# Inverting the key norms as one column per chunk and head in a recurrent-scan kernel, with its helper jobs moved and a fifth job place added

## The chip, the cores and the metric

The kernel runs as one launch on one core of a Trainium2 chip, all arithmetic in fp32. The metric is the device time of that launch in microseconds (us), the median over the runs shown. The engines are called TensorE (PE in the profile; PEld is its weight load), VectorE (DVE), ScalarE (ACT), GpSimd (POOL) and SyncE (SP, which issues most DMAs).

## The reference, cut to what matters

One layer of a hybrid backbone over 128 context and 1024 latent tokens (1152 in all) of width 1024: a modulated RMSNorm and an input projection, two parallel mixers (RWKV-7 scans in both directions, and a pooling mixer), an output projection, an expert-choice mixture of 16 experts, a last norm. The change is in the scans:

```python
kk = heads(k * k_k)
kk = kk / jnp.maximum(jnp.sqrt(jnp.sum(kk * kk, axis=-1, keepdims=True)), 1e-12)
k_dir = heads(k[:, :, None, :] * (1.0 + (a - 1.0) * k_a))
...
sa = jnp.einsum('bhvk,bhk->bhv', s, kk_t)
s = (s * w_t[:, :, None, :] - sa[..., None] * b_t[:, :, None, :]
     + v_t[..., None] * k_t[:, :, None, :])          # b_t = kk * a
```

`kk` is the key of each token and head (8 heads of 64), divided by its own length: one number per token and head, shared by 64 channels.

## The kernel before, in words

Five phases run one after the other, with a barrier between them: `project_phase` (to about 405 us of the span), `scan_phase` (about 405 to 1168), `output_phase`, `expert_phase` (the long one) and `final_phase`. Only `scan_phase` is touched.

**Layout.** Channels lie on partitions: a *channel tile* t (0 to 3) is 128 partitions = 2 heads of 64, with the 1152 tokens in the free dimension, worked on in three *pieces* c of 384 tokens (`piece(c)`). Two big buffers, `wide` and `set1`, hold the prepared tensors of even and odd tiles (`bufs(t)`), so that tile t+1 is prepared while tile t is scanned.

**The scan rounds.** The scan is done by chunks of 64 tokens (`CH`); 128 tokens are a *cell*, 9 cells per tile, 36 in all, done two at a time in 18 *rounds* p = 0 to 17. The engines have hand-written programs in which each round has the same skeleton: a triangular matrix is inverted in six levels, `lv` = 0 to 5. Per level and cell TensorE does `inv_x`, ScalarE copies it (`take_x`, L1038), TensorE does `inv_t`, and VectorE adds it to `tw` (`take_t`, L1249 for level 0, L1254, and L1257 for level 5). GpSimd makes the masked matrix of each level (`level`, L882) and `tw` at the round's start (`begin_tt`, L889). Between the levels stand the other steps of the two old cells (`wu`, `fin`, `step`, `y0`) and the first ones of the two next (`ab`, `masked`, L1239).

**The side work.** Three lists fill the gaps of the rounds. *Jobs* are matmuls of 384 columns with their evictions, at up to four places (`spot(p, k)`, k = 0 to 3: places 0 and 1 in level 4, 2 and 3 in level 5); `jobs(p, k)` says which. `between(p, q)` on VectorE, ScalarE and GpSimd holds the element-wise steps after level q. The preparation of tile t = 1, 2, 3 begins in round `PREP[t]` = 0, 4, 8 and takes rounds r = 0 to 3 counted from there, so that rounds 1, 5, 9 are its r = 1, rounds 2, 6, 10 its r = 2, rounds 3, 7, 11 its r = 3. The output norm of tile 0, 1, 2 begins in round `NORM[t]` = 6, 10, 14. Tile 0 is prepared in a *prologue* ahead of round 0 (p = -1), and tile 3 is normed in a *tail* (`TAIL`). A job's PSUM banks are G[0] and G[1]; TensorE waits for all earlier evictions before a job (`evicted`), and once more at the next round's start before `wu`.

**The key norm before**, per piece: ScalarE squares k (`square`, L991); job `kk` sums the squares of each head with a block of ones, so that the sum stands in all 64 rows of the head; ScalarE takes the square root (L999) into a 128x384 tile in `kr[:, 1, 1]`; VectorE bounds it from below (`floor`, L1189), inverts all 128x384 numbers (`unit`, L1197), multiplies key, k_k and inverse (L1199), and multiplies the rate pair `nb` by it (L1202). In the rounds `floor` stands at (r, q) = (1, 5), (2, 1), (2, 4) and `unit` at (2, 2), (2, 3), (2, 5). Behind them: the exponentials (`exps`, L1009 to L1015, two halves per piece at (2, 3), (2, 4), (2, 5), (3, 1), (3, 2), (3, 3)), VectorE's `keys` (L1215, L1216) and `factors` (L1226 to L1234), GpSimd's `kr` (L901), `kd` (L894) and `bonus` (L907, L909). The output norm has a like step, `spread` (L1209), a reciprocal of 128x384.

## Time and profile before

| | us |
|---|---|
| median of 3 runs (lowest, highest) | 3024.35 (3022.92, 3027.27) |
| the profiled execution, own time | 3028.03 |
| its span, first to last instruction | 3026.2 |
| TensorE busy in the span | 2715.8 (90%) |
| VectorE busy | 1214.7 (40%) |
| ScalarE, GpSimd busy | 568.8, 569.1 (19% each) |
| mean granted TensorE clock | 0.956 of 2.4 GHz |

The page gives busy sums over the whole span. The scan phase is a quarter of it, so its share is read from windows of the trace: busy time of each engine in a stretch, and how long a round lasts.

### The profile page before, as it was taken

The numbers are of one execution on the slowest core, as the hardware profiler recorded it, in microseconds if no ns is written. First come the engines' busy times: TensorE is split into PE (matmuls) and PEld (weight loads), VectorE is DVE, ScalarE is ACT, GpSimd is POOL, SyncE is SP. The second block draws the span as 40 slices with busy tenths as digits, with TensorE's granted clock in tenths as the row PEclk, the third lists the DMA queues.
The fourth block names the chain that finished last, engine by engine and source line by source line (L and its number), as shares of the span: only waits on it lengthen the run. The fifth ranks groups of instructions, "written<-read, shape, count | busy, mean of one in ns | idle before, by whom it ended". The sixth has DMA issues, their size and how long they took to land. (4 is left out here: it accounts for less than half of the span.)

```text
span 3026.2 us, 74869 instructions
## 1 busy us (share of the span) xinstructions
PE 2715.8 (90%) x32716; PEld 2389.9 (79%) x32716; DVE 1214.7 (40%) x3032; ACT 568.8 (19%) x1406; POOL 569.1 (19%) x571
## 2 busy tenths in 40 slices
...
DMA packets 235257, 517.92 MB, mean 171 GB/s; under 512 B 9853, under 2 KB 42877, under 8 KB 234938
## 3 DMA queue, kind: packets, MB, share of 16 engines
...
## 5 line engine op out<-in xcount | busy, mean ns | idle before, releaser
L2275 PE MATMUL ps_h<-xT,w1c 128*128 128x144 f32 x4096 | 547.1, 287 | 1.3 <-ACT xT L2081 1.3
L2275 PE MATMUL ps_h<-xT,w3c 128*128 128x144 f32 x4096 | 544.3, 286 | 0.0
L2275 PEld LDWEIGHTS ps_h<-xT,w1c 128*128 128x128 f32 x4096 | 520.4, 191 | 1.7 <-ACT xT L2081 1.7
L2275 PEld LDWEIGHTS ps_h<-xT,w3c 128*128 128x128 f32 x4096 | 519.9, 190 | 0.0
L2285 PE MATMUL ps_ye<-he,w2c 128*128 128x144 f32 x4096 | 512.3, 286 | 0.0
L2285 PEld LDWEIGHTS ps_ye<-he,w2c 128*128 128x128 f32 x4096 | 505.9, 190 | 0.0
L2230 DVE TENSOR_TENSOR u<-ps_h,sig 128x144 f32<-128x144 f32 x256 | 78.8, 308 | 887.8 <-ACT sig L2112 887.8
L563 PE MATMUL front_bank<-wide,win 128*128 128x384 f32 x912 | 298.9, 490 | 2.0 <-DVE wide L447 2.0
L563 PEld LDWEIGHTS front_bank<-wide,win 128*128 128x128 f32 x912 | 173.8, 191 | 128.2 <-issue 9.9
L2112 ACT ACTIVATE sig<-ps_h 128x144 f32<-128x144 f32 x256 | 74.4, 291 | 1065.8 <-PE ps_h L2275 1065.8
L2143 POOL DMA_INDIRECT acc<-ys,idx_s x16 | 25.8, 1615 | 1002.8 <-ACT ye_p L2101 872.0
L882 POOL TENSOR_TENSOR lm<-am,cst 128x256 f32<-128x256 f32 x216 | 164.7, 782 | 261.9 <-DVE am L1239 155.2
L1413 PE MATMUL bank<-xw,tw 64*64 64x64 f32 x2304 | 147.1, 221 | 28.6 <-ACT xw L1038 13.8
L1413 PE MATMUL bank<-tw,xw 64*64 64x64 f32 x2880 | 166.3, 220 | 6.4 <-issue 5.3
L1254 DVE TENSOR_TENSOR tw<-bank,tw 128x512 f32<-128x512 f32 x144 | 98.8, 690 | 181.0 <-PE bank L1413 180.7
L1413 PEld LDWEIGHTS bank<-tw,xw 64*64 64x64 f32 x2880 | 150.3, 137 | 14.7 <-issue 11.2
L1413 PEld LDWEIGHTS bank<-xw,tw 64*64 64x64 f32 x2304 | 131.4, 136 | 37.3 <-ACT xw L1038 18.2
L2137 POOL DMA_INDIRECT xs<-h,idx_s x17 | 17.0, 1001 | 706.0 <-DVE idx_p L2200 706.0
L1413 PE MATMUL bank<-tw,lm 64*64 64x64 f32 x2880 | 114.9, 225 | 28.5 <-DVE tw L1249 16.1
L1413 PEld LDWEIGHTS bank<-tw,lm 64*64 64x64 f32 x2880 | 105.7, 141 | 37.1 <-issue 32.5
L2181 DVE TENSOR_SCALAR_CACHE_REDUCE after<-prow,pcol 128x128 f32<-128x128 f32 (+2 forms) x153 | 115.6, 756 | 0.1
L487 DVE SCALAR_TENSOR_TENSOR mod_sum<-ada,silu_c,mod_sum 128x512 f32<-128x512 f32 x112 | 106.7, 953 | 5.5 <-DVE mod_sum L487 1.6
...
## 6 DMA issues: line engine op xcount, KB each, us to landing
...
```

Of the source, the lines that this page charges most:

```text
L487: mc(eng.scalar_tensor_tensor(out, ada[:, h, k], c, out, ALU.mult, ALU.add))
L563: ins = eng.matmul(ps_p[b][c][:, 0:PIECE], win[:, b, k], hT[:, k, c * PIECE:(c + 1) * PIECE], start=(k == 0), stop=(k == KT - 1))
L882: eng.tensor_tensor(lm[:, b, lv % 2].rearrange("p (d h) c -> p d h c", d=2), am[:, n % 4, :, :, 2], lvl[:, :, lv].unsqueeze(2).to_broadcas ...
L1254: ins = eng.tensor_tensor(flat, INV[b][:], flat, ALU.add)
L1413: return eng.matmul(out, a, b, start=start, stop=stop, skip_group_check=True)
L2112: eng.activation(sig[:, f % 2], ps_h[f % 2][:, 0:SLOTS], ACT.Sigmoid).then_inc(sig_done, 1)
L2137: eng.indirect_dma_start(xs[:], None, io["h2"], bass.IndirectOffsetOnAxis(ap=idx_s[:, 0], axis=0)).then_inc(gathered, 16)
L2143: eng.indirect_dma_start(io["acc"], bass.IndirectOffsetOnAxis(ap=idx_s[:, 1], axis=0), ys[:], None, compute_op=ALU.add).then_inc(scattered ...
L2181: eng.tensor_scalar(after[:, 0:hi - me], prow[:, me:hi], p, None, ALU.is_gt, ALU.add, accum_out=cnts[:, t, 1:2])
L2230: eng.tensor_tensor(u[:, f % 2], ps_h[f % 2][:, 0:SLOTS], sig[:, f % 2], ALU.mult).then_inc(u_done, 1)
L2275: ins = eng.matmul(ps_h[g % 2][:, off:off + SLOTS], w[:, b, k, f * P:(f + 1) * P], xT[:, k], start=(k == 0), stop=(k == KT - 1))
L2285: ins = eng.matmul(yps(k), w2c[:, b, f, k * P:(k + 1) * P], he[:, b, f], start=(c == 0 and f == 0 and k % 3 == 0), stop=(c == NCHUNK - 1 a ...
```

## The change

**Norm.** A new job `ks`, one per tile, replaces the three `kk`: 36 matmuls, each with the squares of one chunk and head as stationary 64x64 operand and one column of ones as moving operand, so that the sums of a chunk stand as one column of 64. ScalarE takes two roots of 128x9 into `rt` (128x2x9), VectorE bounds and inverts `rt` once (`invert`). Job `kb`, one per piece, spreads the inverses back: 12 matmuls whose stationary operand is one column of `rt` repeated 64 times and whose moving operand is `eye`. `unit` then multiplies key, k_k and the PSUM result in two instructions of 128x192, and `nb` as before. The squares go to `kr[:, 0, 1]` or, for t > 1, to `kdt`.

**Places.** A round gets a fifth place, `spot(p, 4)`, after place 3, on banks G[2] and G[3]. The jobs, `kd`, `kr`, `exps`, `normed`, `deviation` and `spread` move as the diff shows. `spread` becomes three reciprocals of 128x128.

```diff
         if p == -1:
-            for lo, name, t in ((0, "w", 0), (3, "a", 0), (6, "kk", 0), (9, "w", 1)):
+            for lo, num, name, t in ((0, 1, "ks", 0), (1, 3, "w", 0), (4, 3, "a", 0), (7, 3, "kb", 0), (10, 3, "w", 1)):
...
-            if r == 0 and k < 3 and t > 1:
-                found.append(("w", t, k))
-            for name, spots in (("a", ((0, 3), (1, 0), (1, 1))), ("kk", ((1, 2), (1, 3), (2, 0))),
-                                ("bonus", ((3, 1), (3, 2), (3, 3)))):
+            spots = {"ks": ((0, 0),), "w": ((0, 1), (0, 2), (0, 3)) if t > 1 else (), "a": ((1, 0), (1, 1), (1, 2)),
+                     "kb": ((1, 3), (2, 0), (2, 1)), "bonus": ((3, 1), (3, 2), (3, 3))}
...
-            e = 4 if t < 2 else 2
-            gate = ((3, 2), (3, 3), (5, 0)) if t < 2 else ((3, 0), (3, 2), (3, 3))
-            for name, spots in (("mean", ((0, 2), (0, 3), (1, 0))), ("var", ((1, 1), (1, 2), (e, 1))), ("gate", gate)):
+            spots = {"mean": ((0, 2), (0, 3), (1, 0)), "var": ((1, 1), (1, 2), (2, 4)),
+                     "gate": ((3, 4), (3, 4), (4, 4)) if t < 2 else ((3, 2), (3, 3), (3, 4))}
...
@@ gpsimd, between @@
-                if (r, q) in ((1, 1), (1, 5), (2, 0)):
-                    kd(t, ((1, 1), (1, 5), (2, 0)).index((r, q)))
-                if (r, q) in ((2, 5), (3, 1), (3, 3)):
-                    kr(t, ((2, 5), (3, 1), (3, 3)).index((r, q)))
+                if (r, q) in ((1, 4), (1, 5), (2, 0)):
+                    kd(t, ((1, 4), (1, 5), (2, 0)).index((r, q)))
+                if (r, q) in ((2, 4), (3, 0), (3, 2)):
+                    kr(t, ((2, 4), (3, 0), (3, 2)).index((r, q)))
...
-                spots = ((2, 0), (2, 1), (5 if t < 2 else 3, 0))
+                spots = ((2, 1), (2, 3), (3, 2))
                 if (r, q) in spots:
                     normed(t, spots.index((r, q)))
@@ scalar, between @@
-                if (r, q) in ((1, 3), (1, 4)):
-                    for c in ((0,), (1, 2))[q - 3]:
-                        square(t, c)
-                spots = ((2, 3), (2, 4), (2, 5), (3, 1), (3, 2), (3, 3))
+                if r == 0 and q <= 3:
+                    square(t, q - 1)
+                spots = ((2, 2), (2, 3), (2, 4), (2, 5), (3, 1), (3, 2))
...
-                spots = ((0, 5), (1, 1), (3, 5) if t < 2 else (2, 1))
+                spots = ((0, 5), (1, 1), (2, 3))
                 if (r, q) in spots:
                     deviation(t, spots.index((r, q)))
@@ vector @@
-        def floor(t, c):
-            x = bufs(t)[0][:, 1, 1, piece(c)]
-            eng.wait_ge(job_s, taken[("kk", t, c)])
-            eng.tensor_scalar(x, x, 1e-12, None, ALU.max).then_inc(floor_v, 1)
+        def invert(t):
+            eng.wait_ge(job_s, taken[("ks", t, 0)])
+            eng.tensor_scalar(rt[:], rt[:], 1e-12, None, ALU.max).then_inc(floor_v, 1)
+            eng.wait_ge(floor_v, 2 * t + 1)
+            eng.reciprocal(rt[:], rt[:]).then_inc(floor_v, 1)
...
             eng.wait_ge(kd_p, 3 * t + c + 1)
-            eng.wait_ge(floor_v, 3 * t + c + 1)
-            x = kr[:, 1, 1, piece(c)]
-            eng.reciprocal(x, x).then_inc(unit_v, 1)
-            eng.wait_ge(unit_v, 9 * t + 3 * c + 1)
-            eng.scalar_tensor_tensor(kx, kx, head(t, "k_k"), x, ALU.mult, ALU.mult).then_inc(unit_v, 1)
-            eng.wait_ge(unit_v, 9 * t + 3 * c + 2)
+            eng.wait_ge(job_p, order_pe[("kb", t, c)])
+            k3 = kx.rearrange("p (b c x) -> p b c x", c=2, x=CH)
+            for m, b in enumerate(bank_of("kb", t, c)):
+                eng.scalar_tensor_tensor(k3[:, :, m], k3[:, :, m], head(t, "k_k"), b[:, 0:PIECE // 2].rearrange("p (b x) -> p b x", x=CH),
+                                         ALU.mult, ALU.mult).then_inc(job_v, 1)
...
-            eng.reciprocal(x, x).then_inc(spread_v, 1)
+            for j in range(3):
+                ins = eng.reciprocal(x[:, j * P:(j + 1) * P], x[:, j * P:(j + 1) * P])
+            ins.then_inc(spread_v, 1)
...
-                spots = ((1, 5), (2, 1), (4 if t < 2 else 2, 5))
+                spots = ((1, 5), (2, 2), (3, 1))
                 if (r, q) in spots:
                     spread(t, spots.index((r, q)))
@@ tensor, job @@
+            elif name == "ks":
+                eng.wait_ge(square_s, 3 * t + 3)
+                for j in range(NCH):
+                    for h in range(2):
+                        ins = mm(b[h][H[j % 2], j // 2:j // 2 + 1], squares(t)[H[h], j * CH:(j + 1) * CH], blk[H[h], h * HS:h * HS + 1])
+            elif name == "kb":
+                eng.wait_ge(floor_v, 2 * t + 2)
+                for j in range(NB // 3):
+                    for m in range(2):
+                        for h in range(2):
+                            i = c * (NB // 3) + j
+                            ins = mm(b[m][H[h], j * CH:(j + 1) * CH], rt[H[m], h, i:i + 1].to_broadcast([HS, HS]), eye[H[m]])
@@ tensor, spot @@
-            else:
+            elif k < 4:
                 evicted(p, k)
                 if k == 0:
                     eng.wait_ge(d_s, 2 * p + 2)
+            else:
+                eng.wait_ge(am_v, min(2 * p + 4, NCELL))
```

Two places show how the instructions move. First VectorE in round 2 (r = 2 of tile 1, buffer `set`), from the step that follows `take_f` of the second old cell to the end of the round. `zs` is the scan state, `am` the masked matrix of a next cell. Before:

```order
L1197 RECIPROCAL set<-set 128x384
L1199 SCALAR_TENSOR_TENSOR z<-z,par,set 128x384
L1202 SCALAR_TENSOR_TENSOR set<-set,z 128x2x384
L1287 SCALAR_TENSOR_TENSOR zs<-bank,fc,mrn 128x64 x2
L1254 TENSOR_TENSOR tw<-bank,tw 128x512 x2
L1239 TENSOR_TENSOR am<-bank,cst 128x2x256 x2
L1197 RECIPROCAL set<-set 128x384
L1199 SCALAR_TENSOR_TENSOR z<-z,par,set 128x384
L1202 SCALAR_TENSOR_TENSOR set<-set,z 128x2x384
```

The same place in the changed program:

```order
L1300 SCALAR_TENSOR_TENSOR zs<-bank,fc,mrn 128x64 x2
L1267 TENSOR_TENSOR tw<-bank,tw 128x512 x2
L1252 TENSOR_TENSOR am<-bank,cst 128x2x256 x2
L1267 TENSOR_TENSOR tw<-bank,tw 128x512 x2
L1300 SCALAR_TENSOR_TENSOR zs<-bank,fc,mrn 128x64 x2
L1209 SCALAR_TENSOR_TENSOR z<-z,par,bank 128x3x64 x2
L1213 SCALAR_TENSOR_TENSOR set<-set,z 128x2x384
L1252 TENSOR_TENSOR am<-bank,cst 128x2x256 x2
L1209 SCALAR_TENSOR_TENSOR z<-z,par,bank 128x3x64 x2
```

Levels 2 and 3 have lost their `unit`; two units stand together in level 4, and (2, 5) has none in the diff.

Second, GpSimd in round 3 (r = 3 of tile 1), from `begin_tt` (`tw<-lm,cst`) on; `lm` are the levels' matrices, `set<-set,z` is `kr`, `kdt<-kdt` begins `bonus`. Before:

```order
L889 TENSOR_TENSOR tw<-lm,cst 128x4x64 x2
L882 TENSOR_TENSOR lm<-am,cst 128x256 x2
L901 TENSOR_TENSOR set<-set,z 128x2x384 x2
L882 TENSOR_TENSOR lm<-am,cst 128x256 x2
L907 TENSOR_TENSOR kdt<-kdt 128x384
L909 TENSOR_TENSOR kdt<-kdt,z 128x384
L882 TENSOR_TENSOR lm<-am,cst 128x256 x2
L901 TENSOR_TENSOR set<-set,z 128x2x384 x2
L882 TENSOR_TENSOR lm<-am,cst 128x256 x2
```

The changed program:

```order
L898 TENSOR_TENSOR tw<-lm,cst 128x4x64 x2
L910 TENSOR_TENSOR set<-set,z 128x2x384 x2
L891 TENSOR_TENSOR lm<-am,cst 128x256 x4
L910 TENSOR_TENSOR set<-set,z 128x2x384 x2
L916 TENSOR_TENSOR kdt<-kdt 128x384
L918 TENSOR_TENSOR kdt<-kdt,z 128x384
L891 TENSOR_TENSOR lm<-am,cst 128x256 x4
```

Both `kr` stand one step earlier: the first now ahead of the matrices of level 2, the second and a `bonus` ahead of those of level 4.

## Rows read from the trace of the kernel before

Each row of a window gives the stretch in us from the span's start, its length, the busy us of each engine with the number of instructions, the mean granted TensorE clock as a share of 2.4 GHz, and DMA. The rounds' bounds are the starts of their first `take_t` (L1249).

**Rows 1.** Windows: rounds 2, 3, 5, 6, 7, 10, 11 and 12
```profile
534.30:570.80 36.50, 29.51 (x1011) 27.59 (x1006) 29.84 (x54) 19.13 (x46) 16.15 (x17) 1.00 0.02 4
570.80:613.30 42.50, 34.36 (x994) 31.06 (x996) 26.64 (x57) 11.81 (x36) 26.13 (x25) 0.88 0.01 3
...
648.00:687.60 39.60, 31.68 (x997) 28.99 (x994) 27.32 (x56) 16.71 (x40) 15.86 (x16) 0.96 0.04 10
687.60:727.50 39.90, 31.01 (x1020) 28.43 (x1015) 30.94 (x56) 19.54 (x47) 19.04 (x21) 1.00 0.02 4
727.50:773.70 46.20, 35.69 (x1016) 31.15 (x1016) 29.67 (x57) 15.78 (x43) 24.18 (x23) 0.89 0.01 3
...
848.40:889.00 40.60, 31.14 (x1008) 28.24 (x1002) 32.61 (x57) 19.79 (x47) 17.20 (x19) 1.00 0.03 6
889.00:936.60 47.60, 36.98 (x1018) 31.92 (x1018) 30.27 (x59) 15.83 (x43) 27.65 (x27) 0.89 0.02 4
936.60:967.20 30.60, 27.64 (x982) 26.55 (x984) 16.05 (x40) 8.53 (x28) 14.19 (x19) 1.00 0.02 4
```
**Rows 2.** Timeline, seam of rounds 6 and 7: VectorE's last unit, TensorE's next matmul
```profile
722.63 2.54 DVE L1197 RECIPROCAL wide<-wide 128x384 f32<-128x384 f32 x1
...
728.02 1.54 PE L1413 MATMUL bank<-tw,lm 64*64 64x64 f32 x29 [3.23 <-DVE tw L1249]
```
**Rows 3.** Windows of 4 us in round 7
```profile
728.00:732.00 4.00, 3.98 (x115) 4.00 (x117) 0.21 (x1) 0.77 (x2) 0.12 (x1) 0.57 0.02 4
...
760.00:764.00 4.00, 2.22 (x8) 1.10 (x10) 3.44 (x8) 0.00 (x0) 2.40 (x4) 0.50 0.00 0
```
**Rows 4.** Groups by line and form, 250 to 1150 us: busy, mean ns of one
```profile
L1197 DVE RECIPROCAL wide<-wide 128x384 f32<-128x384 f32 x6 | 15.3, 2543 | 0.0
...
L999 ACT ACT_TABLE_LOAD x7 | 9.0, 1283 | 0.1
...
L1319 DVE SCALAR_TENSOR_TENSOR z<-bank,z 128x384 f32<-128x384 f32 x10 | 5.5, 550 | 3.7 <-PE bank L1413 3.7
...
L1199 DVE SCALAR_TENSOR_TENSOR z<-z,par,wide 128x384 f32<-128x384 f32 x6 | 5.0, 833 | 0.2
```
**Rows 5.** Timeline, prologue: VectorE's norm steps, GpSimd's `kr`, TensorE's start of the scan
```profile
429.71 0.89 DVE L1189 TENSOR_SCALAR wide<-wide 128x384 f32<-128x384 f32 x3
...
442.87 1.34 DVE L1199 SCALAR_TENSOR_TENSOR z<-z,par,wide 128x384 f32<-128x384 f32 x1
...
437.75 8.12 POOL L901 TENSOR_TENSOR wide<-wide,z 128x768 f32<-128x768 f32 x4 [13.77 <-ACT wide L1015]
446.97 4.73 POOL L901 TENSOR_TENSOR wide<-wide,z 128x768 f32<-128x768 f32 x2 [1.09 <-ACT wide L1015]
...
455.27 1.98 PE L1413 MATMUL bank<-wide 64*64 64x128 f32 x32 [4.28 <-DVE wide L1216]
```
**Rows 6.** Timeline, round 7, levels 3 and 4: ScalarE, GpSimd, VectorE, TensorE
```profile
746.22 0.56 ACT L1011 ACTIVATE wide<-wide 128x384 f32<-128x384 f32 x1
...
752.20 5.07 POOL L901 TENSOR_TENSOR wide<-wide,z 128x768 f32<-128x768 f32 x2 [4.11 <-ACT wide L1015]
...
755.52 1.80 DVE L1226 COPY rk_b<-par 128x64 f32<-128x64 f32 x1
...
759.56 1.28 DVE L1254 TENSOR_TENSOR tw<-bank,tw 128x512 f32<-128x512 f32 x2
...
761.78 1.54 PE L1413 MATMUL bank<-kdt,rk_b 64*64 64x384 f32 x4 [5.13 <-DVE z L1319]
```
**Rows 7.** Timeline, end of round 5: `centre` beside `kd`, a `kk` job behind a root
```profile
677.59 3.11 DVE L1179 TENSOR_TENSOR wide<-wide,ht 128x384 f32<-128x384 f32 x2
...
678.17 2.12 POOL L894 TENSOR_TENSOR kdt<-kdt,z 128x768 f32<-128x768 f32 x1
...
681.33 0.86 PE L1413 MATMUL bank<-wide,cst 64*64 64x384 f32 x4 [0.93 <-ACT wide L999]
```
**Rows 8.** Small matmuls in round 2, and mean weight load by form (250 to 1150 us)
```profile
539.91 0.68 PE L1413 MATMUL bank<-cst,wide 64*64 64x64 f32 x31
...
L1413 PEld LDWEIGHTS bank<-tw,xw 64*64 64x64 f32 x2880 | 150.3, 137 | 14.7 <-issue 11.2 <-ACT xw L1038 3.2
```

More of the change, by code:

```diff
@@ L703, in piece, with squares @@
         return slice(c * PIECE, (c + 1) * PIECE)
+    def squares(t):
+        return bufs(t)[0][:, 0, 1] if t < 2 else kdt[:, 0]
     def head(t, name):
@@ L801, in scan_phase, with job_banks @@
                 order_pe[job] = len(order_pe) + 1
-    assert len(order_pe) == 7 * CT * 3
-    def job_banks(p, k, name):
+    assert len(order_pe) == 7 * CT * 3 + CT
+    def job_banks(p, k, job):
         if p == -1:
@@ L809, in job_banks @@
             return [G[k % 4]]
-        return [G[1]] if name in ("bonus", "gate") else G[0:2]
+        if k == 4:
+            return [G[2 + jobs(p, k).index(job)]]
+        return [G[1]] if job[0] in ("bonus", "gate") else G[0:2]
     spot_of = {job: (p, k) for p in range(-1, TAIL + 1) for k in range(spots_of(p)) for job in jobs(p, k)}
@@ L1101, in _ @@
         eng.wait_ge(par_v, 1)
-        for k in range(9):
+        for k in range(10):
             spot(-1, k)
@@ L1107, in _ @@
         centres(0)
-        for k in range(9, 12):
+        for k in range(10, 13):
             spot(-1, k)
@@ L1309, in take_job @@
         def take_job(name, t, c):
-            if name in ("w", "a", "kk", "var"):
+            if name in ("w", "a", "ks", "var"):
+                return
+            if name == "kb":
+                unit(t, c)
                 return
```

91 lines of the change are left out of this document (49 added, 42 removed).

## The prediction

> **What bounds the kernel now.** I read the page's busy sums first. TensorE is busy for 90% of the span, but most of that is the expert phase, which the change leaves alone; so the sums say little here. I then cut the scan phase into its rounds [rows 1]. Round 12 carries almost no side work: it lasts 30.6 us, with TensorE busy 27.64 and VectorE 16.05. That is the clean round. Rounds in which a tile is prepared have the same matmuls (994 to 1020 against 982), yet last 36.5 to 47.6 us, and VectorE is busy 26.6 to 32.6 us in them. So there TensorE does not set the time; the inversion's level-by-level chain does, which runs TensorE, ScalarE, TensorE, VectorE, and finds VectorE or GpSimd occupied. The seam of rounds 6 and 7 shows how [rows 2]: VectorE begins a reciprocal at 722.63, two more steps follow, and TensorE idles 3.23 us for the next `take_t`. After such a wait the granted clock is 0.57 of 2.4 GHz in the next 4 us, and 0.50 in the stretch after the second long wait [rows 3]: about 1.2 GHz, so a stall is paid again partly as slow matmuls. The prologue is a plain VectorE chain, closed by TensorE's start at 455.27 behind L1216 [rows 5].
>
> **The change, part by part.** The sum is made against the profiled execution: span 3026.2, own time 3028.03. That is 3.7 us over the median of 3024.35, so I take the difference off the median.
>
> Per tile VectorE loses three reciprocals of 2.543 us [rows 4], three floors of 0.30 (0.89 for three, [rows 5]) and three L1199 of about 0.83 [rows 4]: 11.0 us. It gains six L1209 of 128x192 from PSUM, estimated at 0.4 each (a 128x384 one that reads PSUM takes 0.55, [rows 4]; half the columns cost more than half), and two steps on 18 columns, estimated at 0.4 together: 2.8. Net 8.2 us per tile, 33 in all, most of it in rounds where VectorE is the occupied one.
>
> *Prologue.* Floors, reciprocals and L1199 there are 0.89 + 7.6 + 2.6 = 11.1 us; 2.8 comes back. ScalarE has one table load more ahead of the first sigmoid, 1.28 us [rows 4], and the scans start so much later. VectorE would be 7 us earlier. But GpSimd's six `kr` take 8.12 + 4.73 = 12.85 us [rows 5] and can only begin behind the first exponentials; counted from VectorE's units about 433, plus the two waits for ScalarE, they end near 449. So TensorE starts about 6 us earlier. Taken: -6, ends -3 and -8.
>
> *Rounds 2, 6, 10* (r = 2). VectorE loses 7.6 of reciprocals, 0.6 of floors, 2.5 of L1199 and one L1202 (about 1), and gets four L1209 (1.6): -10 of 29.8 to 32.6 busy. These rounds exceed the clean one by 5.9, 9.3 and 10.0 us, 25 together [rows 1]. VectorE's surplus over round 12 is 14 to 17, so two thirds of it go. If the excess followed it would shrink by 17. I take -9 (2, 3.5, 3.5), nearer to a third: `centre` stays in level 1, ScalarE gets a fourth half of `exps`, and two units with a `masked` between them (about 5 us) now stand in level 4. Ends -3 and -17.
>
> *Rounds 3, 7, 11* (r = 3). The seam stall goes with the unit at (2, 5): 3.23 us in round 7. In level 4 VectorE waits for the last exponentials, then does `keys` and `factors` beside GpSimd's `kr`, and comes to `take_t` at 759.56; its copy of 64 columns takes 1.80 us meanwhile, and TensorE waits 5.13 us for the job behind [rows 6]. The exponentials move up by one place, to where ScalarE finishes about 747. But GpSimd's third `kr` moves up too and takes a `bonus` along, both ahead of the level-4 matrices: 747 + 5 + 2 + 0.7 makes 755 before TensorE can do `inv_x`, and about 758 before VectorE's `take_t`. The middle gains 1.5 us, and the wait behind it 1.3. So -6 for rounds 7 and 11, -3 for round 3, which has no norm beside it: -15, ends -3 and -22.
>
> *Rounds 1, 5, 9* (r = 1). Two `kk` jobs leave with a table load, and with TensorE's 0.93 us wait for a root [rows 7]. One `kb` and a unit come, whose eviction TensorE must wait for before `wu`. Both late `kd` now stand at the round's end, where one already stretches `centre` (two instructions in 3.11 us, [rows 7]). Taken -1 each, -3; ends -6 and +6.
>
> *Rounds 0, 4, 8* (r = 0). `ks` in level 4, a root with its own table load, then a sigmoid's (1.28 each): partly ahead of a `take_x`. Taken +1 each, +3; ends 0 and +6.
>
> *TensorE's work.* 36 + 36 small matmuls per tile replace three `kk` pairs. 31 of 64 columns take 0.68 us with the first one's fill [rows 8], so one per 0.015 us: 1.1 us per tile, and about as much in fills; the `kk` matmuls, 0.86 us for a job [rows 7], 2.6 a tile, were about as long. Taken 0. The Trainium skill (TensorE: Matmul & The Clock Gate, Wait — 56ns, not 53.3ns?) says that matmul starts never come closer than about 25 ns, however few the columns. By that figure the 72 would take 1.8 us a tile, the sum would be 3 us worse, an estimate from that page; the row here stands at 15 ns, so the trace disagrees.
>
> *The rest.* Variance, `spread` and gate of the norms leave the crowded r = 2 and r = 3 rounds; the tail has three reciprocals more in pieces, some 0.1 us a piece. A job at place 4 makes the next round wait for its eviction. Taken +1, ends -3 and +4. SP's loads keep their order and are far ahead.
>
> A second rule bears on the contention. In the rows L1197 always takes 2.54 us, while L1199 with both inputs in SBUF takes 0.62 to 1.34 [rows 4, 5]. The Trainium skill (SBUF — State Buffer, Who interferes with whom) has it that a VectorE instruction with at most one SBUF input does not contend with GpSimd, and one with two does. By that rule the reciprocals never held GpSimd up, and the new L1209, one input in PSUM, cannot be held up by it: an estimate of 0.2 us less for each pair, 2 us in all.
>
> **Sum**: -6 - 9 - 15 - 3 + 3 + 0 + 1 = -29: 3024.35 - 29 = 2995 us, for this case alone 2980 to 3012.
>
> **The rivals.** *GpSimd takes VectorE's place.* For it: the two `kr`, each 2.0 us or more, stand ahead of matrices that TensorE needs, and both `kd` close together at the end of r = 1. Against it: GpSimd is busy only 16 to 27.7 us per round. Then r = 3 gains only half the seam stalls (-5), r = 2 half (-4.5), r = 1 loses 1.5 each (+4.5), the rest stays (-6, +3, +1): -7, 3017. Chance 0.14; half of it faster, half within the bound.
>
> *More than forecast.* The stalls feed on themselves through the clock [rows 3]; if they vanish, the prepared rounds drop near 34 us: r = 2 -15, r = 3 -25, others as above: about -50, 2974. Chance 0.12.
>
> *Slower: the round's seam.* `kb` keeps G[0] and G[1] until VectorE has run its unit, which also waits for `kd`, and place 4 adds waits for a variance or gate; `wu` and all behind it on TensorE stand at that. Nine seams have one or the other: those after rounds 1, 5 and 9 (`kb`) and after 8, 10, 12, 13, 14 and 16 (a variance or gate at place 4). If each costs a stall of 3 us and 2 us at half clock, that is +45: 3040. It decides from 29/9, about 3.2 us a seam. Before, the like wait for a root was 0.93 us. Chance 0.07.
>
> *Slower: the small matmuls do not overlap.* If every one of the 72 per tile stood behind its own weight load of 137 ns [rows 8], that is 9.9 us a tile, 39 in all: 3034. The 0.68 us for 31 speak against it. Chance 0.03.
>
> *No effect*: the freed VectorE time was idle anyway, and prologue and r = 0 cancel. 0.02, 3022.
>
> **How the numbers follow.** About 0.2%, 6 us, is what a measurement of this kernel can tell from no change. The forecast has the remaining 0.62, of which 0.02 lies within 6 us. Faster: 0.60 + 0.12 + 0.07 = 0.79; same: 0.02 + 0.07 + 0.02 = 0.11; slower 0.07 + 0.03 = 0.10. The range goes from the large gain's 2974 to 3020, beyond the GpSimd case; above it lies 0.10 and below it some 0.06 of the large-gain case.
>
> **What would show it.** Right: no VectorE reciprocal of 128x384; TensorE's first `ab` near 449; rounds 6 and 10 near 36, 7 and 11 near 41, 3 near 39; no wait of 3 us for L1262 at the seam; a wait of TensorE for GpSimd's `lm` in level 4 of the r = 3 rounds. Wrong: r = 3 rounds over 45 (GpSimd), rounds 1, 5, 9 over 42 or a clock of half at their ends (the seam), a `kb` job over 1 us (weight loads), or less than 3 us in the prologue.

## The result, and the profile after

| | before | after |
|---|---|---|
| median (runs), us | 3026.44 (6) | 3012.86 (6) |
| ratio, 95% interval | | 0.9956 (0.9944 to 0.9967) |
| profiled execution: time, span | 3028.03, 3026.2 | 3012.83, 3010.1 |
| VectorE busy, us | 1214.7 | 1174.0 |

The change takes 13.6 us, 0.44%. The direction was forecast, and 3012.9 lies in the range, but the forecast gain of 29 us was twice what came. One execution of d_more, the kernel of the last experiment, took 5234.65 us at a granted clock of 0.80 and is left out of its ratio.

Of the signs named ahead, TensorE's first `ab` came at 450.17 (forecast 449), the 3 us wait at the seam is gone, and the wait for `lm` in level 4 is there. The lengths missed: rounds 6 and 10 took 37.35 and 40.62 us (forecast 36), 7 and 11 took 44.66 and 45.04 (41), and 3 took 41.06 (39).

Part 1 of the page after: VectorE has 40.7 us less to do (33 were forecast), and the kernel keeps a third of that.

```profile
PE 2719.3 (90%) x33244; PEld 2402.5 (80%) x33244; DVE 1174.0 (39%) x3052; ACT 559.9 (19%) x1399; POOL 566.4 (19%) x571
```

The rounds after, as windows, in the columns of [rows 1]: rounds 2, 3, 5, 6, 7, 10, 11 and 12.

```profile
529.52:567.48 37.96, 31.20 (x1045) 29.45 (x1042) 19.48 (x48) 15.90 (x45) 16.39 (x17) 0.96 0.01 4
567.48:608.54 41.06, 31.56 (x1009) 29.39 (x1006) 24.51 (x56) 11.87 (x35) 24.02 (x24) 0.96 0.01 3
...
643.53:678.80 35.27, 30.98 (x1022) 28.98 (x1020) 28.45 (x59) 15.58 (x37) 16.25 (x17) 0.96 0.04 11
678.80:716.15 37.35, 31.18 (x1050) 28.78 (x1048) 20.66 (x52) 15.98 (x46) 16.13 (x17) 0.99 0.02 4
716.15:760.81 44.66, 35.27 (x1030) 31.54 (x1026) 27.16 (x58) 15.76 (x42) 26.40 (x26) 0.92 0.01 3
...
835.11:875.73 40.62, 33.42 (x1032) 30.27 (x1030) 21.36 (x54) 16.04 (x45) 16.35 (x17) 0.92 0.03 8
875.73:920.77 45.04, 35.72 (x1030) 32.16 (x1026) 27.16 (x58) 15.75 (x42) 26.40 (x26) 0.92 0.01 4
920.77:950.40 29.63, 28.12 (x986) 26.70 (x988) 15.90 (x43) 9.49 (x30) 14.15 (x19) 1.00 0.02 5
```

In rounds 2, 6 and 10 VectorE lost 10 to 11 us each, as reckoned, and round 2 is longer than before, round 10 as long. Rounds 7 and 11 are 1.5 and 2.6 us shorter. The granted clock of rounds 2 and 10, 1.00 before, is 0.96 and 0.92. The seam stall of [rows 2] is gone: the next row is TensorE's first matmul behind `take_t` of round 7.

```profile
717.59 0.59 PE L1427 MATMUL bank<-tw,lm 64*64 64x64 f32 x13 [0.19 <-DVE tw L1262]
```

Two waits stand in new places. In level 4 of round 7, GpSimd does `kr` and a `bonus` ahead of the four `lm` of levels 4 and 5, as the forecast said, and TensorE waits for them (timeline of GpSimd and TensorE):

```profile
734.42 3.58 POOL L910 TENSOR_TENSOR wide<-wide,z 128x768 f32<-128x768 f32 x2 [8.85 <-ACT wide L1025]
737.96 1.00 POOL L916 TENSOR_TENSOR kdt<-kdt 128x384 f32<-128x384 f32 x1
739.03 1.59 POOL L918 TENSOR_TENSOR kdt<-kdt,z 128x384 f32<-128x384 f32 x1
740.58 3.52 POOL L891 TENSOR_TENSOR lm<-am,cst 128x256 f32<-128x256 f32 x4
742.07 1.86 PE L1427 MATMUL bank<-tw,lm 64*64 64x64 f32 x29 [4.39 <-POOL lm L891]
```

VectorE's `take_t` of that level comes at 747.89, 31.7 us behind the round's start; before it was 32.1. The 4.39 us returns as 4.4 in rounds 3 and 11 as well. In round 2, ScalarE's first exponentials, moved up to (2, 2), stand with a table load ahead of `take_x` of level 3. TensorE waits 1.99 us there; before, it waited 1.73 us one level later, behind the same steps at (2, 3). TensorE in before, then ScalarE and TensorE in after:

```profile
559.12 0.33 PE L1413 MATMUL bank<-xw,tw 64*64 64x64 f32 x4 [1.73 <-ACT xw L1038]
```

```profile
546.42 1.28 ACT L1031 ACT_TABLE_LOAD   x1
547.72 0.23 ACT L1031 ACTIVATE ec<-ht 128x36 f32<-128x36 f32 x1
547.86 0.51 ACT L1019 ACTIVATE set<-set 128x384 f32<-128x384 f32 x1
548.27 0.51 ACT L1020 ACTIVATE set<-set 128x384 f32<-128x384 f32 x1
548.68 0.51 ACT L1021 ACTIVATE set<-set 128x384 f32<-128x384 f32 x1
549.09 0.64 ACT L1048 ACTIVATE xw<-bank 128x256 f32<-128x256 f32 x2
549.51 0.35 PE L1427 MATMUL bank<-xw,tw 64*64 64x64 f32 x4 [1.99 <-ACT xw L1048]
```

### The profile page after: what moved, and what is told of

Its sections match the earlier page's. It is cut to its first block and busy times, and to the rows that moved or that the text cites. A ratio compares the mean times of both kernels' runs of the same rounds, so it can differ in the third digit from the quotient of the medians.

```text
span 3010.1 us, 75949 instructions
## 1 busy us (share of the span) xinstructions
PE 2719.3 (90%) x33244; PEld 2402.5 (80%) x33244; DVE 1174.0 (39%) x3052; ACT 559.9 (19%) x1399; POOL 566.4 (19%) x571
## 5 line engine op out<-in xcount | busy, mean ns | idle before, releaser
L1427 PE MATMUL bank<-tw,lm 64*64 64x64 f32 x2880 | 112.6, 224 | 22.9 <-POOL lm L891 13.2
L1427 PEld LDWEIGHTS bank<-tw,lm 64*64 64x64 f32 x2880 | 103.1, 139 | 30.1 <-POOL lm L891 13.6
L487 DVE SCALAR_TENSOR_TENSOR mod_sum<-ada,silu_c,mod_sum 128x512 f32<-128x512 f32 x112 | 105.2, 939 | 5.5 <-DVE mod_sum L487 1.6
```

Source lines behind the costliest of these rows:

```text
L487: mc(eng.scalar_tensor_tensor(out, ada[:, h, k], c, out, ALU.mult, ALU.add))
L1427: return eng.matmul(out, a, b, start=start, stop=stop, skip_group_check=True)
```

## The experiments

Times are ratios to the kernel before, taken beside it on the same chip. Effects of a few us are small against the spread of single executions, so the profiles are compared by sums over the three rounds of a kind. A round is counted from its first `take_t` to the next round's, so most of the stall of the seam 6/7 lies in round 6 (TensorE idles from 724.79 to 728.02, and round 7 begins at 727.50). "Start" is the first `take_t` of round 0, in us from the span's start.

| kernel | ratio (95%) | start | r=0 | r=1 | r=2 | r=3 | rounds 12-16 |
|---|---|---|---|---|---|---|---|
| before | | 462.0 | 104.2 | 117.1 | 116.9 | 136.4 | 169.1 |
| b_again | | 461.0 | 105.2 | 114.3 | 118.8 | 134.0 | 166.5 |
| b_short_recip | 0.9962 (0.9947-0.9976) | 457.9 | 104.1 | 115.4 | 112.3 | 135.2 | 166.9 |
| b_copy_root | 0.9995 (0.9985-1.0005) | 461.3 | 103.8 | 115.8 | 120.1 | 132.5 | 171.2 |
| b_kd_late | 1.0006 (0.9994-1.0017) | 461.9 | 103.3 | 117.1 | 117.7 | 136.6 | 166.7 |
| b_square_late | 1.0003 (0.9993-1.0014) | 461.7 | 103.2 | 116.3 | 119.1 | 136.5 | 166.2 |
| after | 0.9956 (0.9944-0.9967) | 456.9 | 109.7 | 107.5 | 115.9 | 130.8 | 165.0 |
| a_again | 0.9959 (0.9945-0.9973) | 457.5 | 112.4 | 107.6 | 113.9 | 131.0 | 165.7 |
| a_exps_kr_back | 0.9959 (0.9946-0.9972) | 458.4 | 114.0 | 110.7 | 109.9 | 133.7 | 164.2 |
| a_exps_spread | 0.9951 (0.9937-0.9964) | 456.9 | 108.3 | 109.5 | 109.7 | 131.1 | 164.2 |
| a_kr_first | 0.9945 (0.9932-0.9957) | 452.1 | 108.0 | 109.8 | 110.2 | 131.6 | 163.9 |
| a_kr_back | 0.9913 (0.9900-0.9926) | 457.4 | 112.1 | 109.8 | 115.7 | 118.4 | 163.7 |
| a_kr_recip | 1.0030 (1.0020-1.0039) | 462.1 | 109.3 | 116.2 | 138.0 | 117.7 | 163.6 |
| c_both | 0.9906 (0.9890-0.9922) | 452.6 | 109.4 | 111.2 | 112.6 | 120.0 | 165.3 |
| c_ks_end | 0.9898 (0.9881-0.9915) | 453.5 | 104.9 | 110.7 | 112.7 | 118.6 | 167.2 |
| c_centres | 0.9880 (0.9862-0.9899) | 454.6 | 110.0 | 108.8 | 107.0 | 117.1 | 166.1 |
| d_all | 0.9864 (0.9844-0.9883) | 451.6 | 104.1 | 109.8 | 108.9 | 116.7 | 163.3 |
| d_more_again | 0.9824 (0.9808-0.9839) | 453.3 | 100.3 | 111.2 | 108.5 | 111.7 | 169.6 |

**How much a round moves by itself.** Both kernels were profiled again, unaltered.

> The changed kernel unaltered, once more, beside the three below on one chip. It tells how far a round's length moves between two executions of the same program. If the lengths of rounds follow from the order alone, every round lies within 0.5 us of the first profile (38.0, 37.35 and 40.6 for rounds 2, 6, 10; 41.1, 44.7 and 45.0 for 3, 7, 11) and the time is 3010 to 3015; if the clock adds a part by chance, single rounds move by 1 to 3 us, and only sums over several rounds and the medians can be compared.

> The kernel before unaltered, profiled once more: how far its rounds move by themselves. By the first profile rounds 2, 6, 10 took 36.5, 39.85, 40.6, rounds 3, 7, 11 took 42.5, 46.3, 47.6 and rounds 0, 4, 8 took 35.7, 34.7, 33.8. If the rounds of one kernel move as little as 1 us, and sums of three by 2, the differences read so far stand; if rounds 2, 6, 10 sum to 113 or less, the gain read there was chance.

Before moved by up to 2.8 us in a sum of three rounds, after by up to 2.7. Rounds 2, 6 and 10 move most: a_kr_first left them as they are in after, and their sum is 110.2 against 115.9 and 113.9. So two single profiles tell only a difference of 6 us or more in a sum of three; a smaller one stands where several profiles or the medians agree.

**The reciprocals alone, in the old places.**

```diff
...
-            eng.reciprocal(x, x).then_inc(unit_v, 1)
-            eng.wait_ge(unit_v, 9 * t + 3 * c + 1)
             eng.scalar_tensor_tensor(kx, kx, head(t, "k_k"), x, ALU.mult, ALU.mult).then_inc(unit_v, 1)
+            eng.wait_ge(unit_v, 9 * t + 3 * c + 1)
+            eng.reciprocal(x[:, 0:18], x[:, 0:18]).then_inc(unit_v, 1)
```

> The kernel before, but the key norm's reciprocal runs over 18 columns of 384 and is not used (the norm enters scaled down instead, so the unit keys, and the output, are other numbers). All places stay. Theory places (freed VectorE time was worth what the forecast said, and moved steps gave it back): rounds 2, 6, 10 shorter by 2 to 3.5 us each, rounds 3, 7, 11 by 3 each, the prologue by 3 to 5: 18 to 25 us below before, near 3004. Rival cover (most of the freed time was idle on VectorE anyway): rounds 2, 6, 10 shorter by under 1 us each, the seams of 3, 7, 11 by 2 each, the prologue by 4: 8 to 13 us, near 3016.

0.9962: 11 us, the rival's figure. VectorE loses about 27 us (12 times 2.54 less 0.27). Rounds 2, 6, 10 gain 5.6 of the mean of the two profiles of before (117.9), the prologue 3.6, rounds 3, 7, 11 nothing. The gain of rounds 2, 6, 10 is that of their seams. TensorE's waits there were 2.66, 3.23 and 5.26 us before and are 2.13 (now for GpSimd's `lm`), 0.49 and 2.94, together 5.6 us less, and by the count these stalls lie mostly in rounds 2, 6, 10. TensorE at the seams 2/3 and 10/11, before ([rows 2] has 6/7):

```profile
571.36 1.83 PE L1413 MATMUL bank<-tw,lm 64*64 64x64 f32 x29 [2.66 <-DVE tw L1249]
...
889.51 1.83 PE L1413 MATMUL bank<-tw,lm 64*64 64x64 f32 x29 [5.26 <-DVE tw L1249]
```

And in b_short_recip at all three seams, with the wait in level 4 of round 7, which stays at 5.23 us (5.13 in [rows 6]):

```profile
566.87 1.30 PE L1413 MATMUL bank<-tw,lm 64*64 64x64 f32 x29 [2.13 <-POOL lm L882]
...
720.59 1.05 PE L1413 MATMUL bank<-tw,lm 64*64 64x64 f32 x29 [0.49 <-DVE tw L1249]
...
753.24 1.54 PE L1413 MATMUL bank<-kdt,rk_b 64*64 64x384 f32 x4 [5.23 <-DVE z L1319]
...
877.68 1.05 PE L1413 MATMUL bank<-tw,lm 64*64 64x64 f32 x29 [2.94 <-DVE tw L1249]
```

**`kr` back at its old places.**

```diff
-                if (r, q) in ((2, 4), (3, 0), (3, 2)):
-                    kr(t, ((2, 4), (3, 0), (3, 2)).index((r, q)))
+                if (r, q) in ((2, 5), (3, 1), (3, 3)):
+                    kr(t, ((2, 5), (3, 1), (3, 3)).index((r, q)))
```

> The changed kernel with GpSimd's kr alone back at its old places, (2, 5), (3, 1), (3, 3). Theory places: TensorE's waits of 4.4 us for lm in level 4 of rounds 3, 7, 11 go, and each of these rounds is 2 to 4 us shorter: 3001 to 3007. Rival (the wait only moves: kr and bonus then stand before level 5 and the next round's first matrices): each round within 1 us of 41.1, 44.7 and 45.0, the time 3010 to 3015.

0.9913, an interval clear of after's: 13 us less, by nothing but the places of `kr` on GpSimd. Rounds 3, 7, 11 give 12.5 us. Their windows, with round 7's wait for VectorE's `z` down from 5.13 in [rows 6] to 2.04, and the 4.4 us wait for `lm` gone:

```profile
567.78:604.62 36.84, 30.57 (x1009) 27.84 (x1006) 24.40 (x56) 11.81 (x35) 27.38 (x27) 1.00 0.02 4
...
713.25:755.18 41.93, 34.18 (x1031) 30.75 (x1026) 26.26 (x58) 15.59 (x42) 25.20 (x27) 0.96 0.01 3
...
873.81:913.47 39.66, 32.79 (x1030) 29.43 (x1026) 26.31 (x59) 15.59 (x42) 26.62 (x26) 1.00 0.01 3
```

```profile
745.17 0.86 PE L1427 MATMUL bank<-kdt,rk_b 64*64 64x384 f32 x4 [2.04 <-DVE z L1335]
```

The granted clock of these rounds rises from 0.96, 0.92 and 0.92 to 1.00, 0.96 and 1.00.

**The exponentials back as well.**

```diff
-                spots = ((2, 2), (2, 3), (2, 4), (2, 5), (3, 1), (3, 2))
+                spots = ((2, 3), (2, 4), (2, 5), (3, 1), (3, 2), (3, 3))
```

> The changed kernel with the six halves of exps and kr back at their old places. Theory places: ScalarE's table load and three exponentials no longer stand ahead of take_x of level 3, so rounds 2, 6, 10 lose 2 to 3 us each against the changed kernel; in rounds 3, 7, 11 the last exponentials come a level later and keys waits for them, which gives back about 1 each beside the gain of kr at its old places: 2998 to 3005. Rival (the idle VectorE time is taken by another wait in each): 3010 to 3016, rounds 2, 6, 10 within 1 us of 38.0, 37.35 and 40.6.

0.9959, no gain over after: rounds 2, 6, 10 gain, but rounds 3, 7, 11 are at 133.7, as before, with the 5.1 us wait for `z` back in rounds 7 and 11. So the earlier exponentials carry the gain of rounds 3, 7, 11, and `kr`'s earlier place had cancelled it. My price for the late ones (1 us a round) was too low: it is 5 (133.7 against 118.4, for three).

**Exponentials out of (2, 2) only.** The table load and `ec` stay there. On top of `kr` back and of the next experiment (the two are c_both):

```diff
-                spots = ((2, 2), (2, 3), (2, 4), (2, 5), (3, 1), (3, 2))
-                if (r, q) in spots:
-                    j = spots.index((r, q))
-                    if j == 0:
-                        centres(t)
-                    exps(t, j // 2, j % 2)
+                if (r, q) == (2, 2):
+                    centres(t)
+                spots = ((2, 3), (2, 4), (2, 5), (2, 5), (3, 1), (3, 2))
+                for j in range(6):
+                    if (r, q) == spots[j]:
+                        exps(t, j // 2, j % 2)
```

> As c_both, and the first three exponentials leave place (2, 2): the table load and ec stay there, the halves stand at (2, 3), (2, 4), two at (2, 5), (3, 1), (3, 2). If ScalarE's work ahead of take_x of level 3 costs the r = 2 rounds (waits of 2.2 to 2.6 us, and a clock of half behind them), rounds 2, 6, 10 lose 0.5 to 1.5 us each against c_both: 2 to 4 us in all. Rival (the second half at (2, 5) makes kr and take_x of the next round late): rounds 3, 7, 11 longer by 1 to 2 each, no gain or a loss of 2 us.

0.9880 against c_both's 0.9906, on one chip, with intervals that overlap: about 8 us, 5.6 of them in rounds 2, 6, 10. In round 2 TensorE's wait at that point was 1.99 us and is 0.75, and the clock of the round goes from 0.95 to 1.00. c_both's row, then window, and the same of c_centres:

```profile
545.65 0.33 PE L1432 MATMUL bank<-xw,tw 64*64 64x64 f32 x4 [1.99 <-ACT xw L1046]
```

```profile
526.50:563.62 37.12, 31.17 (x1044) 29.45 (x1042) 19.47 (x48) 15.87 (x45) 14.67 (x15) 0.95 0.02 4
```

```profile
544.32 0.33 PE L1432 MATMUL bank<-xw,tw 64*64 64x64 f32 x4 [0.75 <-ACT xw L1046]
```

```profile
526.84:560.75 33.91, 28.81 (x1030) 27.25 (x1032) 19.34 (x50) 14.93 (x43) 13.82 (x14) 1.00 0.02 4
```

The same edit on the changed kernel alone:

> The changed kernel; only the exponentials leave place (2, 2) (the table load and ec stay there), halves at (2, 3), (2, 4), two at (2, 5), (3, 1), (3, 2); kr stays at its new places. If ScalarE's three exponentials ahead of take_x of level 3 cost rounds 2, 6, 10 the part of the forecast that failed: these rounds sum to 107 to 111 us (114 to 116 with them), 4 to 7 us below the changed kernel, a ratio of 0.9935 to 0.9945. Rival (round sums only move with the clock, or kr at (2, 4) now waits for the exponentials of that place and holds the matrices behind it): within 2 us of the changed kernel, 0.995 to 0.9965.

0.9951, an interval that overlaps after's: in the time, the edit alone shows no clear gain. In rounds 2, 6, 10 all profiles of the table together do show one. With exponentials at (2, 2) the sums are 115.9, 113.9, 110.2, 115.7, 112.6 and 112.7 (a_kr_recip aside); with none there they are 109.9, 109.7, 107.0, 108.9 and 108.5. The two groups don't meet, if only by 0.3 us, and their means differ by 4.7 us.

**The prologue.** VectorE takes `kr` of tile 0, GpSimd none:

(`kr_first` holds the two products of `kr`.)

```diff
         for c in range(3):
             keys(0, c)
+            kr_first(c)
...
-        for c in range(3):
-            kr(0, c)
         for n in range(2):
             level(n, 0)
```

> The changed kernel; only in the prologue VectorE does the six kr of tile 0 itself, one pair behind each keys, and GpSimd none. Beside GpSimd's kr (2.4 us each) every instruction of keys took 2.55 us where it takes 0.95 alone. If the two hold each other up: 12 instructions of 0.95 to 1.0 us instead of six of 2.55, TensorE's first ab 2.5 to 4 us earlier (near 447), the time 3009 to 3010. Rival (another wait closes the prologue, the bonus of GpSimd or the level matrices): ab within 1 us of 450.2 or later, 3012 to 3016.

In after, all six instructions of `keys` run beside GpSimd's six `kr`, and both are slow. GpSimd and VectorE in after, the first of `keys` and the row of `ab`:

```profile
434.91 14.30 POOL L910 TENSOR_TENSOR wide<-wide,z 128x768 f32<-128x768 f32 x6 [10.03 <-ACT wide L1025]
435.06 2.57 DVE L1228 TENSOR_TENSOR wide<-wide 128x768 f32<-128x768 f32 x1
450.17 1.99 PE L1427 MATMUL bank<-wide 64*64 64x128 f32 x32 [6.29 <-DVE wide L1229]
```

In a_kr_first VectorE does `keys` and `kr` in turn; one of each pair, and `ab`:

```profile
434.59 0.95 DVE L1226 TENSOR_TENSOR wide<-wide 128x768 f32<-128x768 f32 x1
435.46 0.95 DVE L1227 TENSOR_TENSOR wide<-wide,kdt 128x768 f32<-128x768 f32 x1
436.32 1.82 DVE L1232 TENSOR_TENSOR wide<-wide,z 128x768 f32<-128x768 f32 x2
...
445.35 1.98 PE L1432 MATMUL bank<-wide 64*64 64x128 f32 x32 [1.95 <-DVE wide L1232]
```

Twelve instructions on one engine take 10.4 us, where six and six on two took 14.9. `ab` comes 4.8 us earlier; the ratio is 0.9945 against 0.9956 and 0.9959 of the changed kernel, with intervals that overlap.

> The changed kernel with kr of tiles 1 to 3 back at its old places and kr of tile 0 on VectorE. If the two gains are independent, as their places 250 us apart suggest, they add up: 14 to 15 us from the first, 4 to 6 from the second, together 18 to 22 us below the changed kernel on this chip, a ratio of 0.987 to 0.990 to the kernel before. Rival (the first step of round 0 closes on GpSimd's tw, a wait of 4.7 us in round 0, which takes a part back): 0.991.

c_both has 0.9906 against 0.9913 of a_kr_back. In the profiles its scan starts 4.8 us earlier and ends 7.1 us earlier; the medians show 2 us, with intervals that overlap. Of the expected 18 to 22 us below the changed kernel 17.5 came, medians on one chip, and the ratio is the rival's 0.991. But its reason isn't borne out: TensorE's wait for GpSimd's `tw` in round 0 is 4.66 us, as in after (4.67). That the two gains add up is not settled.

**The reciprocals put back, in the new places.** On a_kr_back:

```diff
                 eng.scalar_tensor_tensor(k3[:, :, m], k3[:, :, m], head(t, "k_k"), b[:, 0:PIECE // 2].rearrange("p (b x) -> p b x", x=CH),
-                                         ALU.mult, ALU.mult).then_inc(job_v, 1)
+                                         ALU.mult, ALU.mult)
+                eng.reciprocal(b[:, 0:PIECE // 2], b[:, 0:PIECE // 2]).then_inc(job_v, 1)
```

> The changed kernel with kr at its old places (2998 us beside 3022 for before) and, behind each half of a unit's first product, a reciprocal of 128x192 in PSUM in its own place, which nothing needs: VectorE gets back about 2.6 us per unit, 31 us in all, with the places as they are. If VectorE's relief made the gain, most of it goes: 15 to 25 us slower than with kr back alone, a ratio of 0.996 to 1.0. If the relief falls mostly into idle time of VectorE and the gain comes from the earlier exponentials and norm keys: 5 to 12 us slower, a ratio of 0.993 to 0.995, of which 4 to 6 in the prologue.

1.0030: 35 us slower for 24 instructions of 1.356 us, 33 us. Rounds 2, 6, 10 pay 22.3 us for the 12 that stand there, 16.3 us of work. Their windows:

```profile
537.15:582.55 45.40, 35.55 (x1040) 33.98 (x1038) 25.44 (x53) 15.72 (x45) 16.34 (x17) 0.84 0.01 3
...
693.61:738.83 45.22, 35.73 (x1050) 32.35 (x1048) 26.66 (x56) 16.14 (x46) 16.39 (x17) 0.84 0.01 3
...
856.24:903.64 47.40, 35.92 (x1040) 31.57 (x1038) 27.19 (x57) 16.48 (x45) 16.45 (x17) 0.87 0.03 8
```

So a microsecond of VectorE is not one price. Behind `take_t` of levels 2, 3 and 5, where `unit` stood, 20 us removed gave 5.6. In level 4, where the units now stand one behind another with `masked` between and TensorE's jobs waiting for their banks, 16 us added cost 22, with the clock at 0.84. In level 4 TensorE waits 2.62 us ahead of the second `kb` in each of the three rounds, where a_kr_back has no such wait; behind `take_t` of level 5 in round 2 it waits 3.64 us (1.68 in a_kr_back). TensorE in round 2 of a_kr_recip:

```profile
570.66 0.58 PE L1428 MATMUL bank<-cst,rt 64*64 64x64 f32 x24 [2.62 <-issue]
...
578.76 1.97 PE L1428 MATMUL bank<-cst,lm 64*64 64x64 f32 x32 [3.64 <-DVE tw L1271]
```

The size is beyond even the first theory's, but its reason is not borne out: taking the reciprocals out of the old places had given a third of this. The edit also keeps the jobs' banks longer, so it doesn't price VectorE's time alone.

**`ks` later.** On c_both, `ks` at place 3 of rounds 0, 4, 8, `invert` at (1, 1):

```diff
-            spots = {"ks": ((0, 0),), "w": ((0, 1), (0, 2), (0, 3)) if t > 1 else (), "a": ((1, 0), (1, 1), (1, 2)),
+            spots = {"ks": ((0, 3),), "w": ((0, 0), (0, 1), (0, 2)) if t > 1 else (), "a": ((1, 0), (1, 1), (1, 2)),
...
-                if (r, q) == (0, 5):
+                if (r, q) == (1, 1):
                     invert(t)
```

> As c_both, and ks stands at place 3 of rounds 0, 4, 8 instead of place 0 (w one place earlier each), invert at (1, 1) instead of (0, 5), the bonus of tile 0 one place earlier. Rounds 4 and 8 were 34.7 and 33.8 us before and 36.4 and 38.0 with kr back. If the root with its table load in level 4 costs that, rounds 0, 4, 8 are 1 to 2 us shorter each against c_both: 2 to 5 us in all. Rival (the root at the seam makes wu wait through the next round's first place): 0 to 6 us longer, with a wait of TensorE for ScalarE's rt at the start of rounds 1, 5, 9.

The rounds give 4.5 us (109.4 to 104.9), the ratio 0.9898 against 0.9906, within the intervals. The other profiles bear the rounds out: with `ks` at place 0 rounds 0, 4, 8 sum to 108.0 to 114.0 in nine of them, with `ks` at place 3 to 104.9, 104.1 and 100.3 (which has a further edit in round 0). In after, round 8 ended with the variance's root at place 4 and a table load for it, and TensorE's `wu` waited; in c_ks_end the load ahead of `ks`'s root serves both, and this wait is gone. After:

```profile
794.61 1.28 ACT L1011 ACT_TABLE_LOAD   x1
...
796.54 1.96 PE L1427 MATMUL bank<-toks,tw 64*64 64x128 f32 x32 [1.49 <-ACT gt L1011]
```

**Rounds 1, 5, 9**, on the kernel before: no square root (`ACT.Copy, scale=100.0` for `ACT.Sqrt`); `kd` of piece 0 at (1, 4) for (1, 1); a square at (1, 4) for (1, 3), another at (1, 5) for (1, 4).

> The kernel before with the key norm's square root left out (Copy of 100 times the sum of squares in its place, so the unit keys and the output are other numbers): no table load for a root in rounds 1, 2, 5, 6, 9, 10 and the prologue, everything else in place. If the roots' table loads made rounds 1, 5, 9 long (38.4 us on average before, 36.1 after), those rounds are 1.5 to 2.5 us shorter each and the prologue by 2 to 3: 8 to 12 us in all, a ratio of 0.996 to 0.9975. Rival (rounds 1, 5, 9 were long by the squares ahead of take_x of level 4 and by VectorE's part in level 2, not by the loads): rounds 1, 5, 9 within 0.7 us of before, 2 to 4 us in all from the prologue, 0.9985 or more.

> The kernel before, with kd of piece 0 at (1, 4) instead of (1, 1), as the change has it, and nothing else. In round 5 it takes 1.80 us at 650.98 on GpSimd, right ahead of the matrices of level 2, and VectorE's take_t of the second cell then comes 2.4 us behind the first instead of 0.9. If that is the unforeseen gain: rounds 1, 5, 9 shorter by 1.5 to 2.5 us each (they sum to 108 to 111 instead of 114.3 to 117.1), a ratio of 0.9975 to 0.9985. If not: 113 or more, 0.9995 to 1.001.

> The kernel before, with the square of piece 0 at (1, 4) instead of (1, 3) and that of piece 2 at (1, 5), so that ScalarE has 0.6 us less ahead of take_x of level 4. If the squares made rounds 1, 5, 9 long: 0.6 to 1.5 us each, these rounds sum to 111 to 113, a ratio of 0.9985 to 0.9995. If not: within 1 us of 114.3 to 117.1 in sum, 0.9995 to 1.001.

Three times no difference: 0.9995, 1.0006, 1.0003, and sums of 115.8, 117.1 and 116.3. None of the three alone is what these rounds gained. The traces show a part of it. Ahead of the second `kk` job of these rounds TensorE waited 0.93, 0.93 and 3.29 us before, the last in round 9. Ahead of `kb` it has no such wait; behind it `wu` waits 2.10 us at the end of round 9. That is 3 of the 8 us. Without the root, 0.93 us went in rounds 1 and 5, and the wait for `take_t` behind it grew by 1.1 us. The wait of 3.29 us stood beside two gate jobs, which moved to place 4, so it needn't be the `kk` job's own. The cause stays open: the `kk` jobs with their `floor`, the places of the `a` jobs and gates, or the three together; that wasn't tried. TensorE in round 9, before and after:

```profile
841.90 1.54 PE L1413 MATMUL bank<-set,cst 64*64 64x384 f32 x4 [3.29 <-issue]
```

```profile
833.58 1.96 PE L1427 MATMUL bank<-toks,tw 64*64 64x128 f32 x32 [2.10 <-issue]
```

**The sum, and two waits more.** d_all holds all four edits; d_more also has `factors` at (2, 3) instead of (3, 3), and tile 0's `bonus` behind the level matrices of round 0.

> kr of tiles 1 to 3 at its old places, kr of tile 0 on VectorE, the exponentials out of place (2, 2), ks at place 3 with invert at (1, 1): the sum of the four edits. If they add: 2 to 4 us below the version without the last edit, a ratio of 0.986 to 0.988. If the round's length is set by the clock's steps rather than by the waits, no further gain: 0.988 to 0.989.

> As d_all, with two waits removed that both kernels had: factors at (2, 3) instead of (3, 3), where it stood 2.7 us ahead of take_t in level 4, and the three bonus of tile 0 on GpSimd behind the level matrices of round 0 instead of ahead of the first tw, for which TensorE waits 4.7 us. If both lie on the path: round 0 shorter by 3 to 5 us, rounds 3, 7, 11 by 1 to 2 each, 6 to 10 us in all, a ratio of 0.983 to 0.986. Rival (the bonus jobs in levels 4 and 5 of round 0 then wait for GpSimd, and level 4 of the others for the exponentials): under 3 us.

```diff
-                if (r, q) == (3, 3):
+                if (r, q) == (2, 3):
                     factors(t)
...
-        for c in range(3):
-            bonus(0, c)
...
+            if p == 0 and q in (1, 2, 3):
+                bonus(0, q - 1)
```

d_all: 0.9864, within what was expected if the edits add. d_more: 0.9817 (0.9800 to 0.9833) and, run again for the profile shown here, 0.9824 (0.9808 to 0.9839): 2970 and 2977 us, the fastest version. Windows of rounds 0, 3, 7 and 11 of d_more_again: round 0 takes 30.10 (35.5 in d_all), the wait for `tw` of 4.66 us gone, and rounds 3, 7, 11 stand at full clock and near 37 us, the wait for `z` of 2.04 us in rounds 7 and 11 gone.

```profile
453.31:483.41 30.10, 26.47 (x824) 24.79 (x826) 11.00 (x20) 9.23 (x23) 16.98 (x22) 0.90 0.02 4
554.02:589.77 35.75, 30.90 (x1008) 28.24 (x1006) 21.95 (x48) 11.82 (x35) 27.34 (x27) 1.00 0.02 4
698.90:737.24 38.34, 32.75 (x1031) 29.35 (x1026) 23.90 (x49) 15.58 (x42) 25.18 (x27) 1.00 0.01 3
847.48:885.07 37.59, 32.89 (x1030) 29.35 (x1026) 23.89 (x50) 15.59 (x42) 26.58 (x26) 1.00 0.02 4
```

Its scan phase ends no earlier than d_all's all the same (VectorE's last instruction of it at 1117.4 and 1117.0): in this execution the scan starts 1.7 us later, and rounds 12 to 16 take 169.6 us against 163.3. Why is not shown.

## Why the prediction was right in direction and wrong in size

Its terms against the means of the two profiles of each kernel:

| term | forecast | measured | with the edits that undo a move |
|---|---|---|---|
| prologue | -6 | -4.3 | -9.4 (a_kr_first) |
| rounds 0, 4, 8 | +3 | +6.3 | -0.6 (d_all) |
| rounds 1, 5, 9 | -3 | -8.2 | -5.9 (d_all) |
| rounds 2, 6, 10 | -9 | -2.9 | -10.9 (c_centres) |
| rounds 3, 7, 11 | -15 | -4.3 | -18.1 (c_centres) |
| small matmuls | 0 | in the rounds | |
| the rest | +1 | -2.0 | |
| sum | -29 | -15.4 | |

The spans' means differ by 14.8 us, the medians by 13.6, so the table accounts for the result.

- **The step that failed** is the term of rounds 3, 7, 11 with that of rounds 2, 6, 10: -24 forecast, -7 measured. I saw that GpSimd's `kr` would stand ahead of the level-4 matrices, and reckoned its end well (755 for round 7 of before, so 27.5 us behind the round's start; TensorE resumed at 25.9). But I kept 6 us of gain for round 7 beside it: the vanished seam stall (3.23), 1.5 in the middle and 1.3 for the wait behind it. Round 7 gained 1.5: 0.3 up to `take_t` of level 4, about 1.2 behind it. The seam stall was no saving for it. By the rounds' bounds that stall lies mostly in round 6, in the excess of which the term of rounds 2, 6, 10 had already taken its third; I counted it twice. b_short_recip shows this: 5.6 us of seam waits go, rounds 2, 6, 10 are 5.6 shorter, and rounds 3, 7, 11 stay. Those are set by the chain of exponentials, `keys` and level 4: the exponentials' place gives 5 us a round, and `kr`'s new place took 4 back. With `kr` in its old places rounds 3, 7, 11 are 16.8 us shorter than before, where 15 were forecast.
- **Rounds 2, 6, 10**: that two thirds of VectorE's surplus over the clean round went didn't matter; taking it by thirds was no measure. Of the work taken out behind `take_t` in the old places (20.5 us), 27% came off the time. In the changed kernel 0.19 us is left of each of the three seam waits, 11 us in all before, and the rounds are only 3 shorter; other waits and the lower clock took the rest. The fourth half of `exps`, which I named but did not price, is a part of it: 4.7 us between the means with and without exponentials at (2, 2).
- **Rounds 1, 5, 9** gave -8.2, not -3. I counted one wait of 0.93 us ahead of a `kk` job and missed the one of 3.29 in round 9. Most of this gain has no shown cause. It is luck for the forecast: with its -3 here the sum would be -10, near the rival's -7.
- **GpSimd takes VectorE's place** was a rival at 0.14 with 3017 us. Rounds 3, 7, 11 came out at its -5, rounds 2, 6, 10 near its -4.5. It was the better account of these six rounds, though it gave no term for the exponentials. Its +4.5 for rounds 1, 5, 9 was wrong, which are at -8.2.
- **The prologue** was nearly right, and GpSimd's `kr` did end at 449.2, where I had 449. But TensorE's `ab` was released by `keys`, 0.8 us later. What I did not count is that `keys`, now wholly beside it, slows from 0.95 to 2.55 us. The reciprocal that ran beside `kr` before had not been held up (2.54 us at 440.30).
- **Rounds 0, 4, 8** cost twice my +3. With `ks` at place 3 they stand at 104.9 and 104.1, as before (104.7).
- **The small matmuls** overlap: `kb`, 12 matmuls, is the 24 records in 0.58 us below (a_kr_back, round 6), so the rival of single weight loads is out. I took the pitch of 0.015 us from records and counted matmuls, of which each has two; `ks` takes 1.23 us in round 0 and three `kb` 1.7, so 3.0 us a tile against 2.6 for the `kk`. L1209 took the 0.4 us estimated for it (0.73 for two).
- **The seams**: of the nine named, `wu` waits at two: 1.49 us behind round 8 and 2.10 behind round 9, where two gates at place 4 follow the `kb`. Both are below the 3.2 us a seam which that rival needed.
- **The clock**: the window 760 to 764 of [rows 3] does not lie behind the second wait, as I wrote, but holds its last 1.8 us (TensorE resumes at 761.78).

```profile
704.82 0.58 PE L1427 MATMUL bank<-cst,rt 64*64 64x64 f32 x24 [0.15 <-issue]
```
